# Score levels of a chunked linear-attention step: strips of 64 key columns by 32 query columns at two row ranges, in place of 32 by 16 at four

## What is computed

```python
b = jnp.cumsum(gc, axis=2)
diff = b[:, :, :, None, :] - b[:, :, None, :, :]
decay = jnp.where(causal, jnp.exp(jnp.where(causal, diff, 0.0)), 0.0)
scores = jnp.einsum('bhtk,bhsk,bhtsk->bhts', qc, kc, decay)
o = o_inter + jnp.einsum('bhts,bhsv->bhtv', scores, vc)
```

## Time and profile before

| | us |
|---|---|
| median of 3 runs | 1082.59 |
| lowest and highest | 1082.35, 1083.51 |
| the profiled execution, its own time | 1080.87 |
| its span, first to last instruction | 1079.1 |
| PE busy | 1051.9 (97%) |
| DVE busy | 674.0 (62%) |
| ACT busy | 478.9 (44%) |
| level steps with 16 moving columns, prompt part: PE busy | 20.1 |
| the same, sample part: PE busy | 4.3 |

### The profile page before, as it was taken

One profiled execution on the slowest core, in us unless ns is written; L12 is line 12 of the kernel. 1 busy time (PEld: TensorE's weight loads), 2 busy tenths in 40 slices (PEclk: granted clock), 3 DMA queues, 4 the chain that ended last, 5 costly groups with the idle time before them and its releaser, 6 DMA issues.

```text
span 1079.1 us, 25184 instructions
## 1 busy us (share of the span) xinstructions
PE 1051.9 (97%) x11040; PEld 992.1 (92%) x11040; DVE 674.0 (62%) x978; ACT 478.9 (44%) x760; POOL 69.8 (6%) x87
## 2 busy tenths in 40 slices
PE   7999999999999999999999979799999999999997
PEld 5999999999999999999999858799999999988886
DVE  6265635675526665356664578988888888744644
ACT  6433344632537333445335527644444444633532
POOL 5100003000013000030000020000000000000000
PEclk9999999999999999999999989999999999999999
DMA  6622223623227222245222363042433323422212
GB/s 192 171 65 79 72 57 116 180 61 80 69 61 216 79 61 79 71 125 166 64 61 89 98 200 104 1 117 79 112 84 92 104 80 98 131 85 78 79 59 87
DMA packets 138717, 105.30 MB, mean 98 GB/s; under 512 B 4017, under 2 KB 123825, under 8 KB 138609
## 3 DMA queue, kind: packets, MB, share of 16 engines
q1 hardware_dynamic: 133744, 85.88, 28.0%
q0 software_dynamic: 4864, 17.83, 5.5%
HBM read 91.89 MB, written 11.80 MB: 96 GB/s over the span
## 4 chain that ended last, share of the span: by engine, by line
PE 93%; DVE 3%; ACT 2%; DVEq 1%; ACTq 0%; issue 0%; DMA 0%; SPq 0%
PE ps L255 43%; PE ps L1805 21%; PE ps L1829 13%; PE ps L362 5%; PE ps L1028 2%; PE ps L1059 1%; PE ps L1049 1%; PE ps L1005 1%; PE ps L1061 1%; PE ps L1066 1%; PE ps L1097 1%; PE ps L1042 1%; PE ps L1024 1%; PE ps L1086 0%; PE ps L1012 0%
## 5 line engine op out<-in xcount | busy, mean ns | idle before, releaser
L255 PE MATMUL ps<-x_hi,w_lo_t 128*128 128x288 f32 x1152 | 251.5, 300 | 0.0
L255 PE MATMUL ps<-x_hi,w_hi_t 128*128 128x288 f32 x1152 | 246.1, 295 | 0.0
L255 PE MATMUL ps<-x_lo,w_hi_t 128*128 128x288 f32 x1152 | 246.0, 295 | 0.0
L241 ACT ACTIVATE w_hi_t<-w_raw_t 128x1024 fp32r<-128x1024 f32 x73 | 77.2, 1058 | 307.6 <-PE ps L255 307.3
L245 DVE TENSOR_TENSOR w_lo_t<-w_raw_t,w_hi_t 128x1024 fp32r<-128x1024 f32 x73 | 89.3, 1223 | 169.1 <-ACT w_hi_t L241 168.7
L255 PEld LDWEIGHTS ps<-x_hi,w_lo_t 128*128 128x128 f32 x1152 | 184.0, 189 | 4.3 <-issue 2.5
L255 PEld LDWEIGHTS ps<-x_lo,w_hi_t 128*128 128x128 f32 x1152 | 185.1, 188 | 0.0
L255 PEld LDWEIGHTS ps<-x_hi,w_hi_t 128*128 128x128 f32 x1152 | 185.1, 188 | 0.0
L1805 PE MATMUL ps<-x_hi,w_lo_t 128*128 128x288 f32 x264 | 78.1, 296 | 3.5 <-DVE work L1621 2.4
L1805 PE MATMUL ps<-x_lo,w_hi_t 128*128 128x288 f32 x264 | 77.8, 295 | 0.0
L1805 PE MATMUL ps<-x_hi,w_hi_t 128*128 128x288 f32 x264 | 77.8, 295 | 0.0
(11 more groups left out here) (302 smaller groups left out, 2106.6 us busy)
## 6 DMA issues: line engine op xcount, KB each, us to landing
w_raw_t<-in_w_in_dram SPq DMA_DIRECT2D x73, 512.0 KB, 3.9
merged<-in_w_ffn_in_dram SPq DMA_DIRECT2D x22, 512.0 KB, 5.2
w_raw_t<-in_w_ffn_in_dram SPq DMA_DIRECT2D x22, 512.0 KB, 4.6
w_raw_t<-in_w_ffn_out_dram SPq DMA_DIRECT2D x22, 512.0 KB, 3.7
h_t<-in_x_prompt_dram SPq DMA_DIRECT2D x8, 512.0 KB, 5.1
h_t<-in_state_gla_dram POOLq DMA_DIRECT2D x4, 1024.0 KB, 6.2
h_t<-in_state_hgrn_dram POOLq DMA_DIRECT2D x8, 512.0 KB, 7.9
out_dram<-h_t POOLq DMA_DIRECT2D x4, 1024.0 KB, 6.0
```

The costliest lines, as they stand in the source:

```text
L241: nc.scalar.activation(w_hi_t[:, u % NSPL, 0:nk, :], w_raw_t[:, u % NRAW, 0:nk, :], ACT.Copy).then_inc(w_hi, 1)
L255: m = nc.tensor.matmul(out[:, q, :], w[:, u % NSPL, k, :], x(k, q), start=first and i == 0, stop=last and i == len(todo) - 1)
```

## The change

The branch for L below 32 steps through a chunk by 64 tokens in place of 32 (`WIDE`). A matmul then has 64 stationary columns and 32 moving ones, and its product goes to PSUM partitions 0 to 63 or 64 to 127. Per level the prompt part has 24 matmuls in place of 48, and the sample part (L up to 4) has 3 in place of 6, all three at partitions 0 to 63. Each matmul now also makes products of keys in one 32-token half with queries in the other; these lie in PSUM elements that the masks don't take. Levels 32 and 64, `diag` and all other engines' code are as before.

```diff
+WIDE = 64
...
-                        for t in range(0, C, STRIP):
-                            m = nc.tensor.matmul(s[t:t + STRIP, o + t // 2:o + (t + STRIP) // 2], K[:, h, c * C + t:c * C + t + STRIP],
-                                                 second(Q[:, h, c * C + t:c * C + t + STRIP], L), start=True, stop=True)
+                        for t in range(0, C, WIDE):
+                            m = nc.tensor.matmul(s[t:t + WIDE, o + t // 2:o + (t + WIDE) // 2], K[:, h, c * C + t:c * C + t + WIDE],
+                                                 second(Q[:, h, c * C + t:c * C + t + WIDE], L), start=True, stop=True)
                 if L <= 4:
                     for h in range(3):
                         o = 3 * NC * C // 2 + h * TS // 2
-                        for t in range(0, TS, STRIP):
-                            m = nc.tensor.matmul(s[t:t + STRIP, o + t // 2:o + (t + STRIP) // 2], K[:, h, TP + t:TP + t + STRIP],
-                                                 second(Q[:, h, TP + t:TP + t + STRIP], L), start=True, stop=True)
+                        m = nc.tensor.matmul(s[0:WIDE, o:o + WIDE // 2], K[:, h, TP:TP + WIDE], second(Q[:, h, TP:TP + WIDE], L), start=True, stop=True)
```

## The result

| | before | after |
|---|---|---|
| median, us | 1082.99 (4 runs) | 1095.82 (4 runs) |
| lowest to highest | 1082.35 to 1083.51 | 1095.67 to 1097.2 |
| profiled execution, its own time | 1080.87 | 1095.67 |
| span | 1079.1 | 1093.9 |

The ratio is 1.0127, with a 95% interval of 1.0113 to 1.0141: the change costs 12.8 us. The forecast was 1096.6.

A forecast was written before the change was run, and what follows sets the result against it. TensorE's queue was taken as the bound. Four rounds of three levels at +0.76 us and two at +0.61 gave 9.1 + 4.9 = +14.0 us, on the median 1096.6 us; range 1091 to 1101, a little over 8 in 10.

The forecast's parts named there:

- The bound: Whole kernel: a level step's cost on TensorE's queue is the kernel's cost; TensorE waits for nobody at the 20 level steps.
- The round: Level matmuls: the time a column range takes per record, set by the weight load, goes from 33 to 59 ns.
- The straight line between 32 and 128 columns: 64-column load, not in the trace: interpolated between 33 and 110 ns per record to 59 ns, load 136 ns.
- The rounds: Level steps: 24 rounds in the prompt part and 6 more in the sample part, the same counts before and after.
- rival 3: Level steps: two wide ranges don't load side by side, records stand 59 ns apart; +43 us, 1125 us; chance 0.07.
- "The queue is in order": Sample part, levels 0 to 2: the upper range has nothing to do in its six rounds.
- "load less 77": Weight loads: 77 ns is fixed latency; the remainder, 32, 61 and 114 ns, is what a range can't share.
- rival 1: Level steps: a 64-column load takes no longer than a 32-column one; +0.2 us, 1082.8 us; chance 0.08.
- The tail: Each level's last matmul: 32 moving columns in place of 16, 198 ns in place of 183, about 0.01 us later.
- Rival 2: Level steps: the stream is bound by records, 8.6 ns each, not by ranges; 1073 us, faster; chance 0.04.
- The base: Whole kernel: the median before the change, 1.7 us above the profiled execution's 1080.87 us, to which +14.0 us was added.

The follow-up runs named there:

- two ranges, 16 columns: Changed kernel with 16 stationary and 16 moving columns in the prompt part, three quarters of each block left out, masks zero: 1077.63 us.
- two ranges, narrow: Changed kernel with 32 stationary columns in place of 64, at partitions 0 and 64, same matmul count, masks zero: 1080.56 us.
- 48 columns: Changed kernel with only the first 48 of each 64 stationary columns, same two row ranges, 32 moving columns, masks zero: 1088.05 us.
- 16 moving columns: Changed kernel with 64 stationary columns kept but 16 moving columns in place of 32, masks zero: 1095.8 us.
- whole array: Changed kernel with 128 stationary and 64 moving columns in the prompt part, 12 matmuls a level: 1118.86 us.
- The run with 8 columns: Kernel before with 8 stationary columns in place of 32 in the prompt part, four ranges and 96 records kept, masks zero: 1081.64 us.
- the run with fewer keys: Kernel before with 24 stationary columns at level 3 and 16 at level 4, result whole: 1080.44 us.

## Why the prediction was right, and where it was off

**The bound.** TensorE's queue sets the time and no idle gap absorbed anything: VectorE's waits grew by the 14.0 us that the levels grew by.

**The round.** 59 ns forecast, 58.5 measured; load 136 ns forecast, 138 measured. The straight line between 32 and 128 columns was the guess on which the forecast hung, and from 32 columns up the experiments lie on it; at 16 the round is longer than the 20 that it gives:

| stationary columns | load, ns | round, ns | seen in |
|---|---|---|---|
| 16 | 93 | 25 | two ranges, 16 columns |
| 32 | 112 | 32 | two ranges, narrow |
| 48 | 125 | 45 | 48 columns |
| 64 | 138 | 58.5 | the changed kernel; 16 moving columns |
| 128 | 192 | 110 | whole array |

From 32 to 64 columns the round grows by 0.83 ns a column. The Trainium skill, "TensorE: Matmul & The Clock Gate", "LDWEIGHTS (loading the stationary operand)", gives columns / 1.2 ns, that is 0.83 a column. The runs agree in the slope down to 32 columns; the round itself is some 5 ns longer than the figure (58.5 against 53.3 at 64).

**The rounds.** 24 and 30, side by side on two ranges, with the last six on the lower range alone: the level with a sample part held 1.86 us (1.85 forecast), the other 1.52 (1.5 forecast). The run with the ranges visited apart shows that the turn-by-turn order is what keeps rival 3 away. "The queue is in order", as the prediction has it, is not quite so: records for an idle range started ahead of up to three others. It did no harm to the sum, since the sample part uses one range only and that range was taken without a break.

**A row was overlooked.** The prediction says that no f32 load with 64 columns stands in the trace, but it quotes one itself a few sentences later, of the transposes, with 111 ns. By its own "load less 77" that load would have meant 34 ns, which is rival 1. The matmuls' load of 64 columns lasts 138 ns, so the loads of the transposes are no measure for it. The straight line was drawn between two matmul loads, and so it held.

**The tail was mis-sized.** I took 198 ns for the last matmul, from `diag`, since it has 32 moving columns; it lasts 224. A record grows with the stationary columns too, and `diag` has 32 of them: with 32 moving columns it lasts 197 ns at 32 stationary ones and 224 at 64. That is 20 x 0.03 = 0.5 us missing from the sum. By luck most of it was made up by the half nanosecond too much per round (20 x 25 x 0.5 ns = 0.3 us).

**Rival 2 was dismissed too fully.** The text read 8.6 ns a record as four ranges of 33 ns and nothing else. The run with 8 columns shows a record bound of about 8 ns that lies just as high. It changed nothing for this forecast, since 48 records at 8.1 ns need 0.4 us and the wide loads 1.37. But whoever had gone to narrower loads on that argument would have been disappointed, as I was by the run with fewer keys.

**The base.** The sum gives 1082.59 + 14.0 = 1096.6, 0.8 us more than was measured; the medians lie 12.8 apart. The interval of the ratio reaches from 12.2 to 15.3 us and holds the 13.9 of the timeline. That the time came so close is in part chance: outside the levels the profiles differ by up to 3 us.

## What to carry to other kernels

Merging small f32 matmuls into wider ones halves their number, not their time: while the moving operand is short, what a column range takes for one is the load of its stationary columns, and four narrow ranges in turn load as much in the time of one. Before widening a strip, read two rows: how far apart the starts stand when fewer ranges are in use, and how long the load lasts at the widths that the trace does have. Keep one tile width within a step, and let the queue visit the ranges in turn.

## What the runs showed of the hardware that I had not expected

- A stream over column ranges has at least two bounds: the load (32 ns a round at 32 columns, 58.5 at 64, 110 at 128), and about 8 ns a record, seen with 8, 16 and 24 columns on four ranges. The shortest distance seen between two records of one range is about 25 ns. The floor of about 25 ns in the Trainium skill, "TensorE: Matmul & The Clock Gate", Part 1, would fit that if it is read for each range; for the whole array the trace disagrees, with starts 8 ns apart.
- TensorE starts records of an idle range ahead of ones that stand before them in the program: of three with wide strips visited apart (78.07 to 78.24 us), of two in the kernel before (76.04 to 76.06 us).
- A change of tile width within a step costs 0.1 us: 0.11 from the last 32-column start to the first 64-column one, 0.16 the other way, 0.20 from 128 to 64. The Trainium skill, "TensorEngine Tiling (Array Packing)", "Key Properties", says that changing the mode drains the engine. The runs agree that a switch costs time; in all three, though, the first record of the new width starts 0.06 to 0.07 us before the last one of the old width ends in the profile, whose ends are modelled.
